# A two-layer decoder trunk on one core: heads taken in pairs, outputs turned by head pair, and other orders at three seams

## The reference

```python
for i in range(2):
    h = rmsnorm(x, norm[i]);  x = x + (fox_attention if i == 0 else dilated_attention)(h)
    h = rmsnorm(x, mlp_norm[i]);  x = x + square(relu(h @ w1[i])) @ w2[i]      # 1024 -> 4096 -> 1024
# fox: 16 heads of 64; q, k rmsnormed per head; s = q k^T / 8 + (c_q - c_k), c = cumsum(log sigmoid(gate)); causal softmax
# dilated: three groups (window, dilation) = (128,1), (512,4), (2048,16), each with its own q, k, v of 16 heads and rope on
#   16 of 64 columns; the groups' outputs are merged per head by the softmax of their log-sum-exps; then @ w_out
```

## Time and profile before

| | us |
|---|---|
| three timed runs, median (lowest, highest) | 1559.63 (1558.02, 1560.07) |
| the profiled execution | 1556.66 |
| its span | 1554.9 |

### The profile page before, as it was taken

The page is one execution under the profiler, slowest core; times in us unless marked ns, Lnnn a source line. Parts: engine busy times, 40 slices in busy tenths (PEclk is TensorE's granted clock), DMA queues, the critical chain, the costliest instruction groups (busy, mean ns, idle before and its releaser), DMA issues.

```text
span 1554.9 us, 24762 instructions
## 1 busy us (share of the span) xinstructions
PE 1527.7 (98%) x9284; PEld 1229.9 (79%) x9284; DVE 938.8 (60%) x1658; ACT 704.3 (45%) x1192; POOL 381.9 (25%) x515
## 2 busy tenths in 40 slices
PE   7999999999999999899999999999999999999999
PEld 6777666878888888788878877887877888888887
DVE  4457644547474758645647586655645566565778
ACT  5433344355454545445434344444353453535353
POOL 3301100020111511162427254334711110101010
PEclk9999999999999999999999999999999999999999
DMA  5221110557565656333222322222224466675753
GB/s 167 81 68 55 42 54 2 162 138 186 135 152 154 139 166 119 125 101 87 69 82 83 124 68 69 82 69 83 72 94 137 126 144 189 125 199 108 196 120 90
DMA packets 111600, 173.57 MB, mean 112 GB/s; under 512 B 12688, under 2 KB 45456, under 8 KB 111504
## 3 DMA queue, kind: packets, MB, share of 16 engines
q1 hardware_dynamic: 91904, 134.51, 27.7%
q0 software_dynamic: 17408, 33.56, 13.3%
q10 hardware_dynamic: 2192, 4.20, 0.8%
HBM read 165.89 MB, written 6.36 MB: 111 GB/s over the span
## 4 chain that ended last, share of the span: by engine, by line
PE 88%; DVE 5%; POOL 4%; issue 2%; ACT 1%; DMA 0%; DVEq 0%; POOLq 0%; ACTq 0%
PE ps L620 57%; PE ps L935 18%; PE ps L745 3%; PE ps L691 3%; PE ps L719 3%; PE ps L757 2%; PE ps L659 1%; POOL qrs L1820 1%; PE ps L683 1%; DVE w_l L1320 1%; DVE w_l L1605 1%; DVE x_sb L1665 1%; ACT p_sb L1085 1%; ACT w_h L1008 1%; POOL e_all L1868 0%
## 5 line engine op out<-in xcount | busy, mean ns | idle before, releaser
L620 PE MATMUL ps<-w_h,act_h 128*128 128x512 f32 x768 | 311.2, 405 | 6.8 <-DVE w_l L1320 3.4
L620 PE MATMUL ps<-w_h,act_l 128*128 128x512 f32 x768 | 303.4, 395 | 0.0
L620 PE MATMUL ps<-w_l,act_h 128*128 128x512 f32 x768 | 303.1, 395 | 0.0
L1320 DVE SCALAR_TENSOR_TENSOR w_l<-w_raw,gain_t,w_h 128x512 fp32r<-128x512 f32 x188 | 142.3, 799 | 104.7 <-ACT w_h L1008 104.6
L620 PE MATMUL ps<-act_h,w_h 128*128 128x512 f32 x512 | 200.0, 391 | 2.0 <-DVE w_l L1578 2.0
L620 PE MATMUL ps<-act_h,w_l 128*128 128x512 f32 x512 | 199.5, 390 | 0.0
L620 PE MATMUL ps<-act_l,w_h 128*128 128x512 f32 x512 | 199.4, 389 | 0.0
L1820 POOL TENSOR_TENSOR qrs<-qss,m_half 128x8 f32<-128x8 f32 x64 | 110.4, 1725 | 316.6 <-DVE qss L1366 316.0
L1085 ACT ACTIVATE p_sb<-ps,negmax 128x128 f32<-128x128 f32 (+4 forms) x256 | 88.1, 407 | 209.2 <-DVE negmax L1421 114.3
L620 PEld LDWEIGHTS ps<-w_h,act_h 128*128 128x128 f32 x768 | 152.9, 199 | 36.7 <-issue 9.1
L620 PEld LDWEIGHTS ps<-w_l,act_h 128*128 128x128 f32 x768 | 152.7, 199 | 28.5
(11 more groups left out here) (223 smaller groups left out, 2431.9 us busy)
## 6 DMA issues: line engine op xcount, KB each, us to landing
w_raw<-in_dil_w_in SPq DMA_DIRECT2D x72, 512.0 KB, 3.7
raw<-in_mlp_w SPq DMA_DIRECT2D x64, 512.0 KB, 4.8
raw<-in_mlp_w POOLq DMA_DIRECT2D x48, 512.0 KB, 5.7
w_raw<-in_mlp_w SPq DMA_DIRECT2D x32, 512.0 KB, 4.9
w_raw<-in_fox_w_in SPq DMA_DIRECT2D x22, 512.0 KB, 3.7
p_sb<-in_mlp_w SPq DMA_DIRECT2D x16, 512.0 KB, 5.4
pT_sb<-in_mlp_w SPq DMA_DIRECT2D x16, 512.0 KB, 6.2
w_raw<-in_mlp_w POOLq DMA_DIRECT2D x16, 512.0 KB, 7.0
```

What stands on the lines that cost most here:

```text
L620: return mm(ps_out, lhs[i], rhs[j], start=(k == 0 and term == 0), stop=(k == KT - 1 and term == 2))
L1320: last = v.scalar_tensor_tensor(w_l[u % WR][:, j, :], raw(u)[:, j, :], gain_t[:, norm, k:k + 1], f(w_h[u % WR][:, j, :]), ALU.mult, ALU.su ...
```

## The change

- *Pairs.* In the fox sets and the sets of group 0 (`paired`) TensorE turns the probabilities of both heads in the even tick, then multiplies both with the values, one bank later than before (lag 4 in place of 3); the results of the two heads lie side by side in one PSUM bank, and DVE's `output` waits for both. Turns of q and k move to even ticks where there is room.
- *Outputs by head pair.* `prepare(1 or 4, ...)` turns one head pair (one slice k of the output projection) for all four token tiles; it has one PSUM bank. Seven of eight are done in ticks (`TURN_TICKS`), the eighth behind the step. Filling works by slices of banks 0, 1, 2 (`FILLS`), in other ticks, behind the values.
- *Feed-forward.* DVE's waits for roots and clearing stand ahead of the first addition. The preparation of x for the second feed-forward operand comes a bank earlier (`TURNED_BEHIND`).
- *Behind layer one.* DVE splits units 0, 1 of set 2 after the additions, and ACT and DVE prepare x before units 2, 3; one addition is put off; the second group of turns comes after three products of bank 1.
- *Opening.* SP loads unit 3 before x 1; ACT and DVE share the high part of unit 0, and TensorE's first wait is for half a unit; small products fill its waiting.

```diff
+TURN_TICKS = {1: [2, 4, 6, 8, 10, 16, 22], 7: [2, 4, 6, 8, 10, 14, 18]}
+FILL_TICKS = {1: [8, 10, 12, 14, 16, 18, 20, 21, 22, 23, 24, 25, 26, 27], 7: [6, 7, 8, 9, 10, 11, 12, 13, 14, 15, 16, 17, 19]}
+FILLS = ([(0, k) for k in range(KT // 2)] + [(1, k) for k in range(KT // 2)]
+         + [(b, k) for k in range(KT // 2, KT - 1) for b in range(2)] + [(2, k) for k in range(KT - 1)])
+FILLS_AHEAD = {1: 2, 7: 5}
+TURNED_BEHIND = {3: [(0, 0), (0, 1)], 4: [(0, 2), (0, 3)], 5: [(1, 0)], 6: [(1, 1)], 7: [(1, 2)]}
...
     # SP
-            for what, n in (("x", 0), ("w", 0), ("w", 1), ("w", 2), ("x", 1), ("w", 3), ("x", 2), ("x", 3)):
+            for what, n in (("x", 0), ("w", 0), ("w", 1), ("w", 2), ("w", 3), ("x", 1), ("x", 2), ("x", 3)):
...
     # TensorE: prepare, values
-                    src = x_sb[:, t, c * P:(c + 1) * P] if n in PREP_OF_NORM else o_sb[:, t, c, 1:1 + P]
+                    src = o_sb[:, i, pc % 8, 1:1 + P] if n in PREP_OUT else x_sb[:, t, c * P:(c + 1) * P]
...
-                    pe.wait_ge(o_done, a)
+                    pe.wait_ge(o_done, a - a % 2 if paired(s) else a)
...
     # TensorE: step
-                        if 2 <= a <= nt + 1:
-                            turn_probs(attend, t0 + a - 2)
+                        if not paired(attend):
+                            if 2 <= a <= nt + 1:
+                                turn_probs(attend, t0 + a - 2)
+                            if 3 <= a <= nt + 2:
+                                values(attend, t0 + a - 3)
+                        elif a % 2 == 0:
+                            for odd in range(2):
+                                if 2 <= a <= nt:
+                                    turn_probs(attend, t0 + a - 2 + odd)
+                            for odd in range(2):
+                                if 4 <= a <= nt + 2:
+                                    values(attend, t0 + a - 4 + odd)
                         if proj is None:
-                            out_terms(attend, a)
-                        if 3 <= a <= nt + 2:
-                            values(attend, t0 + a - 3)
+                            for b, k in out_fill(a, attend):
+                                out_terms(attend, b, k)
...
+                        c = out_early(a, attend)
+                        if c is not None:
+                            prepare(1 if attend == 1 else 4, c // 4, c % 4)
...
     # TensorE: set 2, and the opening
-                            if k == 3:
-                                for t in range(4):
-                                    prepare(3, 1, t)
+                        if proj == 2 and b == 1 and k == 1 and term == 0:
+                            for t in range(4):
+                                prepare(3, 1, t)
...
             pe.wait_ge(ident_done, 1)
+            keep_busy(6)
             prepare(0, 0, 0)
             prepare(0, 1, 0)
+            keep_busy(8)
...
     # ACT, last chunk of layer one
+                        elif layer == 0 and q == S4_B22:
+                            split_high(BANK_DIL)
+                            split_high(BANK_DIL + 1)
                         elif layer == 0:
-                            for u in range(2 * (q - 5), 2 * (q - 5) + 2):
-                                split_high(BANK_DIL + u)
-                            if q == A22_T4:
-                                for t in range(4):
-                                    prepare(3, 0, t)
-                                keep(0)
-                                keep(1)
+                            for t in range(4):
+                                prepare(3, 0, t)
+                            split_high(BANK_DIL + 2)
+                            split_high(BANK_DIL + 3)
+                            keep(0)
+                            keep(1)
...
     # DVE: output, step
-                dve.wait_ge(pv_done, a + 1)
+                slots = slice(2 * (a % 2), 2 * (a % 2) + n)
+                dve.wait_ge(pv_done, a - a % 2 + 2 if paired(s) else a + 1)
...
-                        if 4 <= a and SETS[attend][0] == 0 and tl[a - 4][2]:
-                            normalise(attend, tl[a - 4][0])
-                        if 3 <= a <= nt + 2:
-                            output(attend, t0 + a - 3)
+                        lag = values_lag(attend)
+                        if lag <= a < nt + lag:
+                            output(attend, t0 + a - lag)
+                        if SETS[attend][0] == 0:
+                            for b in range(max(a - lag - 1, 0), nt if a == n - 1 else a - lag):
+                                if tl[b][2]:
+                                    normalise(attend, tl[b][0])
...
     # DVE, feed-forward
+                    dve.wait_ge(xrs_done, 2 * layer + 2)
+                    dve.wait_ge(sums_clear, layer + 1)
                     add(i, 0, 0, final)
...
-                        elif layer == 0:
-                            for u in range(2 * (q - 5), 2 * (q - 5) + 2):
-                                split_low(BANK_DIL + u)
-                        add(i, q, 0, final)
                         if final and layer == 0 and q == A22_T4:
+                            split_low(BANK_DIL)
+                            split_low(BANK_DIL + 1)
                             for t in range(4):
                                 prepare(3, 0, t)
+                        add(i, q, 0, final)
                         add(i, q, 1, final)
-
-                dve.wait_ge(xrs_done, 2 * layer + 2)
-                dve.wait_ge(sums_clear, layer + 1)
...
     # DVE, opening
-            for u in range(4):
+            dve.wait_ge(gain_in, 16)
+            dve.wait_ge(raw_first[0], 16)
+            link(v.tensor_scalar(w_h[0][:, 1, :], raw(0)[:, 1, :], gain_t[:, 0, 1:2], None, ALU.mult))
+            dve.wait_ge(wh_done, 1)
+            for j, done in enumerate((first_low, wl_done)):
+                v.scalar_tensor_tensor(w_l[0][:, j, :], raw(0)[:, j, :], gain_t[:, 0, j:j + 1], f(w_h[0][:, j, :]),
+                                       ALU.mult, ALU.subtract).then_inc(done, 1)
+            for u in range(1, 4):
                 split_low(u)
```

More of the change, by code:

```diff
@@ L119 @@
 ALONE = [0, 2]
+TURNS_ALONE = {s: [(2, 6) if s == 0 else (3, 1), (3, 5)] + [(b, 4) for b in range(4, QK_SET + 2)] for s in ALONE}
 def set_bank0(s):
@@ L171, in turns_of_tick @@
         return []
-    return [(s, b - 1) for s, b in banks_of_tick(proj, attend, a - 1) if 1 <= b <= QK_SET]
+    due = [(c + 1, s, b - 1) for c in range(ticks_of_step(attend))
+           for s, b in banks_of_tick(proj, attend, c) if 1 <= b <= QK_SET]
+    if paired(attend):
+        taken = set()
+        for i in reversed(range(len(due))):
+            c, s, b = due[i]
+            if (c + c % 2) not in taken:
+                due[i] = (c + c % 2, s, b)
+            taken.add(due[i][0])
+    return [(s, b) for c, s, b in due if c == a]
 def new_slot(s, h):
@@ L233, in turned_count, with out_early @@
     return sum(turned_by_pe(set_of(b)) for b in range(a + 1))
-def out_early(a):
-    return a // 2 if a % 2 == 1 and a < 2 * NT else None
+def out_early(a, attend):
+    return TURN_TICKS[attend].index(a) if a in TURN_TICKS[attend] else None
 STEPS_FOX = [(0, None), (1, 0), (None, 1)]
@@ L963, in mlp, with keep_busy @@
                 chunk(CHUNKS - 1, True)
+            def keep_busy(times):
+                for _ in range(times):
+                    mm(ps_s[1][:, 0:P], ident[:, :], ident[:, :], start=True, stop=True)
             pe.wait_ge(ident_done, 1)
+            keep_busy(6)
             prepare(0, 0, 0)
             prepare(0, 1, 0)
+            keep_busy(8)
             for n, (proj, attend) in enumerate(STEPS_FOX):
@@ L1121, in step @@
                     if proj is None:
-                        if out_early(a) is not None:
-                            prepare(1 if attend == 1 else 4, 0, out_early(a))
+                        c = out_early(a, attend)
+                        if c is not None:
+                            prepare(1 if attend == 1 else 4, c // 4, c % 4)
                     for s, b in banks_of_tick(proj, attend, a):
@@ L1293, in _ @@
                 step(proj, attend)
-            act.wait_ge(merged, 4 * HS)
-            act.wait_ge(x_out, 16 * NT)
-            for t in range(NT):
-                act.dma_start(x_sb[:, t, :], x_dram[t * P:(t + 1) * P, :]).then_inc(x_back[t], 16)
             out_projection(BANK_DIL_OUT, 4)
@@ L1855, in step @@
                 for a in range(n):
-                    if attend is not None and 3 <= a <= len(ticks_of(attend)) + 2:
-                        merge(attend, TICK0[attend] + a - 3)
+                    lag = values_lag(attend) if attend is not None else 0
+                    if attend is not None and lag <= a < len(ticks_of(attend)) + lag:
+                        merge(attend, TICK0[attend] + a - lag)
                     for s, b in banks_of_tick(proj, attend, a):
```

167 lines of the change are left out of this document (87 added, 80 removed).

## The result

| | before | after |
|---|---|---|
| timed runs, median (lowest, highest), us | 1558.83 (1557.32, 1560.07) | 1580.72 (1579.55, 1583.37) |
| the profiled execution, its span, us | 1556.66, 1554.9 | 1583.37, 1581.3 |
| mean granted TensorE clock | 1.000 | 0.989 |

The ratio is 1.0142, 95% interval 1.0130 to 1.0154: 22 us slower. The sign was forecast, the size was not (1566, range to 1574). What follows is read from these two.

What follows compares the result with a forecast made beforehand. TensorE, busy 98% of the span, was taken as the bound. Terms -6.2 + 13.9 + 7.6 - 2.3 - 4.8 - 2.0 = +6.2 us on 1556.7 gave 1562.9; with 3.0 to the median, 1566, range 1539 to 1574.

Steps and rivals of the forecast that it cites:

- rival E: Clock falls to half in the two steps without projection, 16 pairs some 1.5 us more each: 1590; chance 3%.
- pairing in sets 0 and 4: Where products fill the ticks, one visit less per pair saves 6.8 us, less 0.6 for stalls: -6.2 us.
- the seam: Where the first feed-forward part meets the next set: stalls of 1.6 and 2.6 us go, -4.8 us.
- the two steps: Forgetting set 1 and last set, without projection: longer chain and preparations between the maxima, +13.9 and +7.6 us.
- opening: Start of the kernel: shared high part and small fillers that raise the clock earlier, -2.0 us.
- The chain in the steps without projection: Forgetting set 1 and last set: output waits for both heads' value products, +0.61 us a pair before preparations.
- busy for less than 70%: Sign that the forecast is right: TensorE's busy share in forgetting set 1 falls below 70%.
- DVE's order: Steps without projection: preparations stand before the odd head's maximum, delaying it 1.37 us, or 2.11 behind filling.
- rival C: Outputs wait for both heads, but preparations don't hold the second maximum in the steps without projection: 1545; chance 12%.
- the term +0.6 for stalls: Sets 0 and 4: allowance for stalls from pairing, 0 to +3 us, as each pair of ticks has 3.9 us slack.
- Behind the first feed-forward part: Transition to the next set: reordered splits, additions and x preparation remove two stalls, -4.8 us (bounds -4.8 and -1.7).
- Feed-forward starts: Both feed-forward parts: DVE's wait moves before the first addition, removing 1.0 us of idle time twice, -2.3 us.

Runs made afterwards that it cites:

- e7_busy8: The changed kernel with 8 zero-operand products behind each preparation's turning from tick 4 on, in the two steps without projection: 1568.9 us, ratio 1.0064.
- e11_balance: The change with heads singly and preparations in odd ticks in the two steps without projection, four filling products moved to odd ticks in sets 0 and 4: 1539.6 us.
- e9_no_open_fill: The change with heads singly and preparations in odd ticks in the two steps without projection, without the opening's 14 small filling products: 1544.5 us.

## Why the prediction was wrong, point by point

- **The rival E, and that the forecast left it out.** This step failed. It was argued from one idle stretch of 3.1 us at full clock that 2.9 us of idle time in every pair would not lower the clock, and was given 3%. The trace of the change has nine falls, eight products behind each preparation from tick 4 on take them all away, and with them 11.8 us. A single stretch said nothing of a row of them; and two stretches of nearly the same length (1.58 and 2.60, 1.58 and 2.82) bring a fall in one kernel's trace and none in another's. The Trainium skill ("TensorE: Matmul & The Clock Gate", Why this matters for your kernels) has gaps between bursts of products take the clock back to half. The trace agrees that they do, 0.50 in stretches of 3.4 and 6.8 us; but the gaps that the page warns of are longer than the 2.2 to 2.9 us that did it here, so it would not by itself have forecast the falls.
- **The rest of the sum was less good than 1568.9 against 1566 suggests.** At full clock the same kernel, fillers and all, takes 1568.9. But the 3.0 us between 1562.9 and 1566 were there because the median of the kernel before lies above its profiled execution, and by the 21 runs above it takes such times when it loses the clock, which e7_busy8 does not. Profiled execution against profiled execution, both at full clock, e7_busy8 takes 12.4 us more where 6.2 were forecast. That the two numbers meet is in part luck; most of what is missing is pairing in sets 0 and 4 (2.9 us), the seam (1.0), the two steps (1.1), the end of the kernel (0.8) and the opening (0.3).
- **The chain in the steps without projection** was right. At full clock the pairs of the forgetting set miss the forecast by 0.01 to 0.28 us, and the two steps come to +14.4 and +8.2 us in e7_busy8, against +13.9 and +7.6. The clock's part is 23.3 - 14.4 = 8.9 and 13.8 - 8.2 = 5.6 us of the profiled execution. One sign did not come: TensorE was to be busy for less than 70% there, and in the forgetting set's pairs from tick 4 on it is 74% (48.28 of 65.00 us), part of it being work that lasts longer at half clock.
- **DVE's order** (rival C's opposite) was right: 32.6 us hang on which tick a preparation stands in, of them the forecast's 21.2 and the clock.
- **Pairing in sets 0 and 4** was mis-sized: -3.3 in place of -6.2. The visits were priced rightly; the term +0.6 for stalls was too small. It should have been some +3.5, the upper bound being 3; the waits read from the trace grew by 4.3. It counted the slack of a pair of ticks, but the time goes from the odd tick alone; with four products moved there, 4.1 us come back.
- **Behind the first feed-forward part** -3.8 for -4.8: the gap went, and 0.7 came back in set 2, where a turn waits for GpSimd's rope. The put-off addition costs 0.8 at the end of the kernel, a term that the forecast had not named.
- **Feed-forward starts** (-2.6 read in the trace, 2.0 by taking it away, for -2.3) and **opening** (-1.7 for -2.0) were right.

The best kernel run is e11_balance: the change with heads singly in the two steps without projection, preparations in odd ticks, and four products shifted in sets 0 and 4; 1.15% below the kernel before.

## What to carry to other kernels

On an engine that runs its list in order, ask of every step what stands behind it: the same preparations, seven in each of two steps, cost nothing behind the second maximum and over 20 us ahead of it. Where a change makes TensorE idle again and again for some 2 us (here 1.8 to 2.9), price its half clock too, and if the idle time must stay, put harmless products into it, measured so that they end before the next real one. Before a forecast is set against a median, ask whether the kernel before runs at one clock in all its runs. A count of saved visits is not a gain until the tick that lost them still has the time that the other engines need.

## What the runs showed of the hardware

- Half clock came behind some of the idle stretches of 1.8 to 2.9 us that recur from pair to pair, and once behind two of 1.58 and 2.82 us, but not behind a single one of 3.1 us. Nine such falls cost 14.5 us in the profiled execution. The kernel's four runs differ by 3.8 us (mean clock 0.989 to 0.992), those of e7_busy8 by 0.3.
- The kernel before takes 1556.2 to 1557.2 us at a mean clock of 1.000 (nine runs) and 1558.2 to 1560.0 at 0.997 or 0.998 (twelve runs).
- In the opening the products start every 0.43 us, the pace of half clock, until the record of the clock shows its first rise: at 13.5 us in e9_no_open_fill and 14.9 in the kernel before, at 4.6 to 7.1 where small products run from 1.6 us on. The windows view counts the time ahead of that first entry as 1.00.
- A float32 product of 128x128 with a stationary operand that is not a turning takes two instructions of 0.12 us (3.74 for 32); a turning takes one.
